# A hybrid mixer layer on one NeuronCore: the final projection in two token halves, with the decode steps of two recurrences moved

## The reference

```
h    = rmsnorm(x, norm_w);  proj = h @ w_in        # 520 tokens x 2048, about 60 tiles of 128 columns
xbc, dt, qkv, b, a, q_mem, z = split(proj)
y_ssd = ssd_chunked(conv(xbc), dt, A, B, C, D)     # 16 heads of 64, state 128; prompt and decode
y_gdn = gdn_chunked(l2norm(q), l2norm(k), v, g, beta)   # 8 heads of 128, state 128 x 128
y_mem = softmax(q_mem k_mem / sqrt(128)) v_mem     # 4 heads over 256 memory tokens
y   = concat(headnorm(y_ssd), headnorm(y_gdn), headnorm(y_mem)) * mix_norm_w * silu(z)
out = rmsnorm(x + y @ w_out, final_norm_w)         # 2560 -> 2048
```

## Time and profile before

| | before |
|---|---|
| own time of the profiled execution | 1576.6 us |
| its span, first to last instruction | 1574.8 us |
| mean granted TensorE clock | 0.949 |
| TensorE matmuls busy | 1394.4 us (89%), 10688 |
| weight loads busy | 1332.9 us (85%) |
| VectorE busy | 665.9 us (42%), 991 |
| ScalarE busy | 624.3 us (40%), 1187 |
| GpSimd busy | 440.9 us (28%), 425 |
| moved by DMA | 138.16 MB, mean 88 GB/s |

### The profile page before, as it was taken

One profiled execution on the slowest core, in us unless ns is written; L12 is line 12 of the kernel. 1 busy time (PEld: TensorE's weight loads), 2 busy tenths in 40 slices (PEclk: granted clock), 3 DMA queues, 4 the chain that ended last, 5 costly groups with the idle time before them and its releaser, 6 DMA issues.

```text
span 1574.8 us, 25689 instructions
## 1 busy us (share of the span) xinstructions
PE 1394.4 (89%) x10688; PEld 1332.9 (85%) x10688; DVE 665.9 (42%) x991; ACT 624.3 (40%) x1187; POOL 440.9 (28%) x425
## 2 busy tenths in 40 slices
PE   4789998889989999999998989898975877999993
PEld 3689997869978988989898989898975877999993
DVE  4654343322455252524343433333367556323333
ACT  5364346532544545353535353535322014222221
POOL 1121000001332352526344444444254214011102
PEclk8999998899999999999999999999986689999997
DMA  6114451143211211112121212121135323333322
GB/s 256 40 54 124 144 179 52 51 134 116 59 46 49 81 47 63 55 56 60 50 68 44 66 56 68 56 67 56 56 127 185 112 98 95 122 108 104 123 70 109
DMA packets 38820, 138.16 MB, mean 88 GB/s; under 512 B 4448, under 2 KB 5856, under 8 KB 38448
## 3 DMA queue, kind: packets, MB, share of 16 engines
q1 hardware_dynamic: 30384, 109.80, 22.0%
q10 hardware_dynamic: 8208, 26.22, 4.9%
q0 software_dynamic: 112, 0.50, 0.1%
HBM read 121.25 MB, written 15.24 MB: 87 GB/s over the span
## 4 chain that ended last, share of the span: by engine, by line
PE 71%; DVE 12%; ACT 9%; issue 5%; POOL 1%; DMA 1%; ACTq 0%; DVEq 0%; SPq 0%; POOLq 0%
PE ps L744 33%; PE ps L1045 14%; PE ps L649 14%; PE ps L700 1%; PE ps L704 1%; ACT w_hi L1074 1%; DVE d_st L1794 1%; ACT g_e L1281 1%; PE ps L1016 1%; PE ps L998 1%; DVE conv_u L1503 1%; DVE d_v L1831 1%; PE ps L715 1%; PE ps L895 1%; DVE fin L1894 1%
## 5 line engine op out<-in xcount | busy, mean ns | idle before, releaser
L744 PE MATMUL ps<-h_hi,w_hi 128*128 128x260 f32 x1920 | 432.8, 308 | 54.9 <-issue 27.8
L744 PE MATMUL ps<-h_lo,w_hi 128*128 128x260 f32 x1920 | 397.4, 290 | 0.0
L744 PE MATMUL ps<-h_hi,w_lo 128*128 128x260 f32 x1920 | 396.3, 289 | 0.0
L744 PEld LDWEIGHTS ps<-h_hi,w_hi 128*128 128x128 f32 x1920 | 309.5, 197 | 71.2 <-issue 58.0
L1074 ACT ACTIVATE w_hi<-w_raw 128x512 fp32r<-128x512 f32 x352 | 213.4, 625 | 368.4 <-PE ps L1045 159.7
L744 PEld LDWEIGHTS ps<-h_lo,w_hi 128*128 128x128 f32 x1920 | 308.3, 196 | 0.0
L744 PEld LDWEIGHTS ps<-h_hi,w_lo 128*128 128x128 f32 x1920 | 307.3, 196 | 0.0
L1906 POOL TENSOR_TENSOR w_lo<-w_raw,w_hi 128x512 fp32r<-128x512 f32 x156 | 209.0, 1345 | 341.5 <-ACT w_hi L1074 341.5
L1466 DVE TENSOR_TENSOR w_lo<-w_raw,w_hi 128x512 fp32r<-128x512 f32 x196 | 139.6, 734 | 228.8 <-ACT w_hi L1074 228.5
L1045 PE MATMUL ps<-y_hi,w_hi 128*128 128x260 f32 x640 | 129.7, 284 | 6.2 <-DVE y_lo L1878 3.5
L1045 PE MATMUL ps<-y_lo,w_hi 128*128 128x260 f32 x640 | 129.9, 284 | 0.0
(11 more groups left out here) (357 smaller groups left out, 1947.5 us busy)
## 6 DMA issues: line engine op xcount, KB each, us to landing
w_raw<-in_w_in SPq DMA_DIRECT2D x120, 512.0 KB, 3.5
w_raw<-in_w_out SPq DMA_DIRECT2D x40, 512.0 KB, 3.6
w_raw<-in_w_mem SPq DMA_DIRECT2D x16, 512.0 KB, 3.6
x_t<-in_x_t SPq DMA_DIRECT2D x8, 520.0 KB, 7.5
fin<-in_x_t SPq DMA_DIRECT2D x8, 520.0 KB, 4.6
out_y_t<-fin SPq DMA_DIRECT2D x8, 520.0 KB, 2.7
c_kv<-in_c_k ACTq DMA_DIRECT2D x8, 512.0 KB, 5.0
c_kv<-in_c_v ACTq DMA_DIRECT2D x8, 512.0 KB, 4.1
```

The lines of the kernel that those rows point to most:

```text
L744: last = mm(out[:, hf, :], w, a[:, kk, HALF * hf:HALF * hf + HALF], start=(kk == 0 and j == 0), stop=(kk == KT - 1 and j == 2))
```

## The change

**List.** The output projection runs over 260 tokens at a time: all 16 output tiles for tokens 260 to 519, then all for tokens 0 to 259, to which the decode tokens belong. Each half has its own `fin` and `final`. The weights are loaded and split once for each half (`OUT_N` = 32 in place of 16 output tiles; `N_UNITS` grows by 40). The SSD decode goes beside the heads: `decssd0` after the SSD prompt part, slots 0 and 1 into the first 22 items of head 0's stage, 2 to 4 into head 1's, 5 to 7 into head 2's. The GDN decode goes among the first half's output items, `decnorm` and `decgate` to its end. The z tiles are given out anew, so that the heads 5 and 6 have one more and three follow the last head.

```diff
-for _h in range(GDN_H - 1):
-    TILES += z_tiles(_h, _h + 1) + gdn_tiles(_h + 1)
+Z_AFTER = (1, 2, 3, 4, 5, 7, 9, 13)
+for _h in range(GDN_H):
+    TILES += z_tiles(Z_AFTER[_h - 1] if _h else 0, Z_AFTER[_h])
+    if _h + 1 < GDN_H:
+        TILES += gdn_tiles(_h + 1)
     T_HEAD.append(len(TILES))
...
+    slots = []
+    for i in range(8):
+        if i % 4 == 0:
+            slots.append(("decbc", i // 4))
+        slots += [("decssd", i), ("decssdy", i), ("decssdw", i)]
+    decode = [slots[:7], slots[7:16], slots[16:]]
...
+        if h < len(decode):
+            before = spread(before, decode[h]) if before else decode[h]
+        items += spread(main[:FIRST], before) + spread(main[FIRST:], paced([("gdn", h, s) for s in range(CARRY)]))
+    late = paced([("gdn", GDN_H - 1, s) for s in range(CARRY, GSTEPS)])
+    items += spread(proj_items(first, NTILE - 1), late)
+    turn = []
+    for e in Y_ORDER[:-1]:
+        turn += [("yhi", e), ("ylo", e)]
+    items += spread(proj_items(NTILE - 1, NTILE), turn)
...
+    for n in range(OUT_N):
+        for e in Y_ORDER if n == 0 else range(ET):
+            outs.append(("out", n, e))
+            if n and e in (2, 5, 8, 11):
+                outs.append(("fin", n - 1, (2, 5, 8, 11).index(e)))
+            if n == KT and e == 14:
+                outs.append(("final", 0))
+    where = {22: [("decgdn0",)]}
+    for h in range(GDN_H):
+        where[36 + 32 * h] = [("decgdn", h, 0)]
+        where[50 + 32 * h] = [("decgdn", h, 1)]
+    where[298] = [("decnorm",)]
+    where[310] = [("decgate",)]
```

```diff
+    def w_slot(g):
+        if g < in_units:
+            return g % 2
+        return (in_units % 2, 2, (in_units + 1) % 2)[(g - in_units) % 3]
+    def slot_free_after(g):
+        return g - 1 if g <= in_units else g - 2
...
             elif k == "out" and unit_of(it)[1] in (0, 3):
                 g, b = unit_of(it)
-                split_hi(g + 1, 0 if b == 0 else 1)
+                split_hi(g + 2, 0 if b == 0 else 1)
...
                 for j, (w, a) in enumerate(((hi, y_hi), (hi, y_lo), (lo, y_hi))):
-                    for hf in range(2):
-                        last = mm(out[:, hf, :], w, a[:, SLOT[e], HALF * hf:HALF * hf + HALF],
-                                  start=(e == 0 and j == 0), stop=(e == ET - 1 and j == 2))
+                    last = mm(out_ps(n), w, a[:, e, cols], start=(e == 0 and j == 0), stop=(e == last_e and j == 2))
```

```diff
+            elif k == "decbc":
+                g = it[1]
+                act.wait_ge(*upto("rows_out", 16))
+                if g:
+                    act.wait_ge(*upto("d_outer1", 4))
+                    act.wait_ge(*upto("d_ymul", 4))
...
+                for j in range(2):
+                    rows = bc_rows[2 * j + g].rearrange("b n -> (b n)").unsqueeze(0).to_broadcast([P, DB * P])
+                    act.dma_start(d_bb[:, j, :, :].rearrange("p b n -> p (b n)"), rows).then_inc(sem("bb_in"), 16)
+            elif k == "decssdw":
+                i = it[1]
+                act.wait_ge(*upto("d_new", i + 1))
+                act.dma_start(O["s_ssd"][i], s_st[:, i % 2, :, :]).then_inc(sem(f"out_sst{i % 2}"), 16)
+                if 1 <= i < 7:
+                    slot_load(i + 1)
...
                 if i:
-                    pool.wait_ge(*upto("d_new", i))
+                    pool.wait_ge(*upto("d_yred", i))
                 G.tensor_tensor(d_tmp[:, :, :], d_bb[:, 0, :, :], along(d_k[:, 2, i, :], P), ALU.mult).then_inc(sem("d_outer1"), 1)
```

```diff
-                    A(g_s[:, 5, 0:4], g_s[:, 5, 0:4], ACT.Ln, scale=1.0 / P, bias=eps[:, 0:1]).then_inc(sem("g_yln"), 1)
-                    act.wait_ge(*upto("g_yln", h + 1))
-                    A(g_s[:, 5, 4:8], g_s[:, 5, 0:4], ACT.Exp, scale=-0.5).then_inc(sem("g_yr"), 1)
...
+                    V.tensor_scalar(g_s[:, 5, 0:4], g_s[:, 5, 0:4], 1.0 / P, EPS, ALU.mult, ALU.add).then_inc(sem("g_ms"), 1)
...
+                G.tensor_tensor(g_s[:, 5, 4:8], g_s[:, 5, 0:4], eps[:, 2:3].to_broadcast([P, 4]), ALU.pow).then_inc(sem("g_yr"), 1)
```

More of the change, by code:

```diff
@@ L117 @@
 WORK_SEQ = [n for n, t in enumerate(TILES) if t[0] != "qm"]
-GATES = ((0, 8), (16, 20), (8, 15), (15, 16))
-Y_ORDER = [*range(8), *range(16, 20), *range(8, 16)]
+Y_ORDER = [*range(15), *range(16, 20), 15]
+YLO_POOL = (2, 5, 8, 11, 14, 17)
+YLO_V = [e for e in Y_ORDER if e not in YLO_POOL]
+YLO_G = [e for e in Y_ORDER if e in YLO_POOL]
+OUT_N = 2 * KT
 FIN_V = 10
-N_UNITS = KT + 2 * NTILE + KT * ET // 8
+N_UNITS = KT + 2 * NTILE + OUT_N * ET // 8
 GSTEPS = 30
@@ L245, in timeline @@
         first = T_HEAD[h]
-        before = [("gdn", h - 1, s) for s in range(CARRY, GSTEPS)] if h else []
-        items += spread(main[:FIRST], paced(before)) + spread(main[FIRST:], paced([("gdn", h, s) for s in range(CARRY)]))
-    late = [("gdn", GDN_H - 1, s) for s in range(CARRY, GSTEPS)] + [("decssd0",)]
-    for g in range(SSD_G):
-        late += [("decbc", g)]
-        for i in range(4 * g, 4 * g + 4):
-            late += [("decssd", i), ("decssdy", i)]
-    late += [("decgdn0",)] + [("decgdn", h, s) for h in range(GDN_H) for s in range(2)]
@@ L260, in timeline @@
-    items += [("out", 0, 3), ("yhi", Y_ORDER[-1]), ("out", 0, 4), ("out", 0, 5)]
-    for n in range(KT):
-        for e in range(ET):
-            if n == 0 and e < 6:
-                continue
-            if n == 0:
-                items.append(("ylo", e))
-            items.append(("out", n, e))
-            if n and e in (1, 4, 7, 10):
-                items.append(("fin", n - 1, (1, 4, 7, 10).index(e)))
-    items += [("fin", KT - 1, s) for s in range(4)] + [("final",)]
+        before = paced([("gdn", h - 1, s) for s in range(CARRY, GSTEPS)]) if h else []
@@ new lines, in timeline @@
+        if h < len(decode):
[7 more added lines that the diff above has]
+    items += spread(proj_items(NTILE - 1, NTILE), turn)
+    items += [("post", NTILE - 1, s) for s in range(3)] + [("yhi", Y_ORDER[-1]), ("ylo", Y_ORDER[-1])]
@@ L271, in timeline @@
+    where[310] = [("decgate",)]
+    count = 0
+    for it in outs:
+        items.append(it)
+        if it[0] == "out":
+            items += where.get(count, [])
+            count += 1
+    items += [("fin", OUT_N - 1, s) for s in range(4)] + [("final", 1)]
     return items
@@ L531, in build, with h_used @@
     in_units = tile_units(NTILE - 1)
-    pool_units = range(ring["proj", POOL_TILES[0], 0], ring["proj", POOL_TILES[1], 0])
+    pool_units = list(range(ring["proj", POOL_TILES[0], 0], ring["proj", POOL_TILES[1], 0]))
+    pool_turn = {g: i for i, g in enumerate(pool_units)}
+    dve_turn = {g: i for i, g in enumerate(g for g in range(N_UNITS) if g not in pool_turn)}
     def low_part(g, pieces):
-        if g in pool_units:
-            return sem("w_lo_pool"), 2 * (g - pool_units[0]) + pieces
-        return sem("w_lo_done"), 2 * (g - (len(pool_units) if g > pool_units[-1] else 0)) + pieces
+        if g in pool_turn:
+            return sem("w_lo_pool"), 2 * pool_turn[g] + pieces
+        return sem("w_lo_done"), 2 * dve_turn[g] + pieces
+    def h_used(kk):
+        if kk == KT - 1:
+            return upto("unit_used", in_units)
+        kk = kk + 1 if kk == 7 else kk
+        return sem("h_used"), kk + 1 - kk // 8
     conv_at = {n: i for i, n in enumerate(CONV_SEQ)}
```

455 lines of the change are left out of this document (254 added, 201 removed).

## The result

The changed kernel takes 1531.7 us (median of 4 runs, 1527.5 to 1536.1) against 1566.6 us before: ratio 0.973, 95% interval 0.966 to 0.979. The forecast was 1514 us, range 1475 to 1549. The profiled execution has an own time of 1531.7 us and a span of 1529.9; against the 1574.8 of before that is 44.9 us less, where 52.4 were forecast. The page now has TensorE busy for 1367.3 us (89%), VectorE 737.1 (48%), ScalarE 611.9 (40%), GpSimd 461.1 (30%), and 161.27 MB moved.

A forecast was written before the change was run, and what follows sets the result against it. TensorE, 89% busy, was taken as the bound except in the late stage, bound by the decodes. Terms gave 1479.4 + 29 + 10 + 7 - 3 = 1522.4, 52.4 under the profiled span; from the median 1514 us, range 1475 to 1549.

The forecast's parts named there:

- The main term: Late stage, 168.3 us with both decodes among the last projection tiles, goes; its projection matmuls then take 48.4 us.
- The way into the output: Between last projection tile and first output tile: high copies, weight pieces and low parts cost 7 us (3 to 14).
- Norms: Ln and Exp on ScalarE become a VectorE operation and GpSimd power: 3 us gained (6 gained to 10 lost).
- windows 0 to 2: Stages of heads 0 to 2, holding SSD decode slots: 2 us for the first, others 12.8 and 20.3 before absorbing some 3 each.
- The spreading matmuls: Decode's opening step, moved earlier: 32 small matmuls at 0.128 us cost 4.1 us.
- SSD decode beside the heads: Slots in heads 0 to 2 outlast their windows and delay work queued behind: 29 us lost (5 to 50).
- Ports: Rival: each of GpSimd's 16 decode operations holds up a GDN operation 1.3 us, 21 us more, 1535 us; chance 0.16.
- Output: Output projection: 230.4 us of matmuls, 31.1 GDN decode, 3 small sums, 10 us of disturbance (2 to 35).
- The first half's final: Final scaling at item 335 of the output: VectorE makes no low part for about 10 us; 5 us lost.
- item 22: Output projection: TensorE waits for squares on ScalarE, behind four state-load issues; 3 us.
- The ring: Three raw weight buffers keep up; rivals: late in second half, 1530 us, chance 0.11; slower, 1642 us, chance 0.05.
- Tail: Last output matmul to the end: shorter scalings and final operations save 7.0 us, leaving 19.3 us.

The follow-up runs named there:

- run 5: Changed kernel with two z tiles taken from heads 5 and 6 and given back to the end of the projection: ratio 0.984 to the kernel before.
- run 1: Changed kernel with the SSD heads' norm by Ln and Exp on ScalarE again instead of a GpSimd power: ratio 0.964 to the kernel before.
- run 4: Kernel before with only the attention heads' norm by a power on GpSimd: ratio 0.996 to the kernel before.
- run 3: Changed kernel without the SSD decode in the heads, one small VectorE instruction kept per slot: ratio 0.951 to the kernel before.
- run 8: Kernel of run 1 with the decode's opening step behind the SSD list instead of at its end inside it: ratio 0.963 to the kernel before.
- run 2: Changed kernel with the SSD decode laid evenly over all matmuls of the first three heads, not each one's first 22: ratio 0.969 to the kernel before.
- run 7: Kernel of run 2 with each slot's five large decode instructions standing apart in the list: ratio 0.961 to the kernel before.
- run 6: Changed kernel with the first half's final logarithm three items later and its 16 multiplications two at a time: ratio 0.969 to the kernel before.

## Why the prediction was right, and where it was not

**The main term was right.** The late stage went. With the z tiles where they had been (run 5), tile 44 to the first output matmul took 275.1 us, against the 278.0 of the forecast (390.9 less 112.9), and 840 output matmuls in a row came at 0.122 us each. The forecast's mechanism for the gain, decodes taken from a stage of their own and put beside matmuls, is what the trace shows. The way into the output was right too: from the last tile's first matmul (1216.0) to the first output matmul (1235.1) 19.1 us with 11.5 us of matmuls, 7.6 lost where 7 stood.

**Norms: the step that failed most.** "The power is not in the trace; a small GpSimd operation takes 0.23 us ... above it is bounded by the 2.6 us of two table loads." The bound was none: 3.1 us for 16 columns. It was worth some +15 us beside SSD (run 1), by itself outside the range of 6 gained to 10 lost, and -6 to -10 in the attention stage (run 4); together +5 to +9 where -3 stood. The GDN norms' powers were not tested alone; where nothing else changed (run 3's windows 0 to 2, tiles 36 to 43) the stages take what they took before, so they are worth little. 41 table loads went, not 32. A bound must come from what limits the new operation, not from the price of the one it replaces. That the two signs nearly cancel, and so keep the term inside its range, is luck.

**The spreading matmuls and their place.** Their 4.1 us were 4.0; the half clock behind them, some 1.5 us, was not priced. The larger part of the 11.7 us that run 1 leaves, some 6, is their place in the list: with the step behind the list, the five tiles ahead of it take what they took before (run 8). The forecast moved a step and did not count that all SSD items then stand against other tile matmuls.

**SSD decode beside the heads.** Forecast 29, measured 38.6, inside 5 to 50. The mechanism, in the forecast's words "on ScalarE the copies ... behind its wait for the stored slot", was there: 35.4 us of waits, and GpSimd waited 13.2 us for states, as foreseen. Windows 1 and 2 cost 10.8 and 18.0 us where the sum has 9.8 and 17.3. Window 0 was the step that failed: 2 us stood there, 9.5 came. TensorE has one wait of 8.5 us in it, put down to nothing by the profile, and it ends with the low part that GpSimd makes behind slot 1's outer product, which itself waited for slot 0's reduction, as only one temporary is left:

```profile
563.61 1.89 POOL L2104 TENSOR_TENSOR d_tmp<-d_bb,d_k 128x1024 f32<-128x1024 f32 x1 [2.42 <-DVE y_dec L1893]
565.46 1.26 POOL L2002 TENSOR_TENSOR w_lo<-w_raw,w_hi 128x512 fp32r<-128x512 f32 x1
566.82 0.77 PE L822 MATMUL ps<-h_hi,w_hi 128*128 128x260 f32 x2 [8.51 <-issue]
```

The forecast has this dependence for the later slots, but held that window 0's loads, being early, make it cheap. And of the 38.6, 12.8 are the clock, which the term did not have, so part of the agreement in windows 1 and 2 is luck. Spreading alone (run 2) took away ScalarE's wait and gained only 10; that the rest was queueing on VectorE and GpSimd fits run 7, but no run took one engine's queueing away alone.

**Ports.** The measured 1531.7 us lies nearer to this rival's 1535 than to the forecast's 1514, but its mechanism did not come. It has 16 GDN operations held up by 1.3 us each, 21 us in all. In windows 0 to 2 VectorE's operations that are not the decode's, some 145, took 95.3 us in all without the decode, 96.5 in the changed kernel and 98.8 in run 7; GpSimd's 105 took 109.8, 111.5 and 117.8. Between run 2 and run 7 the decode's price fell from 28.7 to 16.9 us, while the slot's addition on VectorE took 1.38 us on average in run 2 and 1.76 in run 7, and GpSimd's two products 1.90 and 2.01 against 1.90 and 1.96: the meetings became hardly shorter. That they lengthen an addition is seen (1.96 us in the changed kernel, 1.23 for the GDN decode's addition in the output stage). The Trainium skill ("SBUF — State Buffer", "Who interferes with whom") describes an exclusive lock between the two engines; the longer additions agree with it, but no run here took the meetings away, so their share of the remaining 16.9 us is open.

**Output.** 13.1 us over 230.4 + 31.1 + 3, where 10 stood. The decode's matmuls took 1.68 and 1.78 us a head where 1.84 and 2.05 were read the earlier trace rows, 3.4 us less in all; so the disturbance was 16.5. The first half's final was 8.5 of it, not 5 (run 6), 4.7 of them the clock; item 22 was 1.6, not 3; the other 6.4 were not tested. The ring decided one wait of 2.4 us, behind that final, and neither of its two rivals came, though the late one's 1530 us is near the measured time: no landing median was over 7.9 us.

**The gain that was not foreseen.** The z tiles' new places were put at nothing. They were worth 12 us (run 5). This error covers much of those of the other sign, the norms' and the SSD decode's; without it the kernel would have come out at about 1544, near the edge of the range. That the sum is 7.5 us off in the end is luck.

**Tail.** 17.2 against 19.3.

**Range.** The root of squares of 21, 25, 7 and 13 is 35.8 and not 35, so the upper end would have been 1550.

## What to carry to other kernels

Where TensorE is near its full rate, price a wait twice: once as it stands, and once for the granted clock behind it; here a third of what a badly placed block of work cost was the clock (12.8 of 38.6 us). Work laid beside a chain in which each step waits for the one before, on another engine, should stand one instruction at a time: the same instructions cost 38.6 us in blocks and 16.9 one by one. Keeping them away from the step on which the weight preparation hangs gave 4 to 5 us more in one trace, close to what traces differ by. And fill a chain's waits with matmuls from a stretch in which TensorE is the bound; each such tile was worth some 6 us.
